# A decoder trunk on one core: pre-norm statistics by a tile of ones, and an opening of three units

## What is computed

```python
def rmsnorm(x, g):
    y = xf * lax.rsqrt(jnp.mean(xf * xf, axis=-1, keepdims=True) + RMS_EPS)
    return y * g
...
for l in range(DEPTH):
    h = h + 0.5 * rmsnorm(swiglu(rmsnorm(h, g[FFN1_PRE]), ffn_w_in[l, 0], ffn_w_out[l, 0]), g[FFN1_POST])
    hn = rmsnorm(h, g[MIX_PRE])
    ...
    h = h + rmsnorm(merged @ w_o[l], g[MIX_POST])
    h = h + 0.5 * rmsnorm(swiglu(rmsnorm(h, g[FFN2_PRE]), ffn_w_in[l, 1], ffn_w_out[l, 1]), g[FFN2_POST])
```

## Time and profile before

| | us |
|---|---|
| median of three runs | 1187.16 |
| the profiled execution | 1185.94 |
| its span, first to last instruction | 1184.1 |
| PE busy | 1174.6 |
| DVE busy | 727.6 |
| ACT busy | 554.6 |
| POOL busy | 428.5 |

### The profile page before, as it was taken

One profiled execution on the slowest core, in us unless ns is written; L12 is line 12 of the kernel. 1 busy time (PEld: TensorE's weight loads), 2 busy tenths in 40 slices (PEclk: granted clock), 3 DMA queues, 4 the chain that ended last, 5 costly groups with the idle time before them and its releaser, 6 DMA issues.

```text
span 1184.1 us, 23842 instructions
## 1 busy us (share of the span) xinstructions
PE 1174.6 (99%) x9265; PEld 1144.5 (97%) x9265; DVE 727.6 (61%) x1131; ACT 554.6 (47%) x809; POOL 428.5 (36%) x486
## 2 busy tenths in 40 slices
PE   9999999999999999999999999999999999999997
PEld 8999999999999999999999999999999999999986
DVE  5755445968666865544587554458676668755542
ACT  6533335536554643333455333346366546543441
POOL 0955500007212276542108545110073122955500
PEclk9999999999999999999999999999999999999999
DMA  9754357373355355535636553574733653654540
GB/s 324 260 178 155 130 184 221 107 236 98 90 156 187 122 196 171 174 128 183 214 111 213 176 168 120 196 212 132 235 105 90 186 170 120 222 192 159 194 161 35
DMA packets 197998, 198.70 MB, mean 168 GB/s; under 512 B 4368, under 2 KB 190864, under 8 KB 197920
## 3 DMA queue, kind: packets, MB, share of 16 engines
q1 hardware_dynamic: 197600, 197.27, 52.1%
q10 hardware_dynamic: 320, 0.34, 0.1%
HBM read 196.54 MB, written 1.05 MB: 167 GB/s over the span
## 4 chain that ended last, share of the span: by engine, by line
PE 94%; issue 3%; DVE 1%; ACT 1%; DMA 1%; POOL 0%; SPq 0%; DVEq 0%; ACTq 0%; POOLq 0%
PE bank L525 27%; PE bank L526 27%; PE bank L524 27%; PE bank L761 2%; PE bank L763 2%; PE bank L762 2%; PE bank L850 1%; PE bank L845 1%; DVE w_lo L1295 1%; PE bank L804 1%; PE bank L559 1%; PE bank L558 1%; DMA raw<-in_ffn_w_in 1%; PE bank L815 0%; PE bank L653 0%
## 5 line engine op out<-in xcount | busy, mean ns | idle before, releaser
L524 PE MATMUL bank<-x_hi,w_hi 128*128 128x272 f32 (+1 forms) x1993 | 574.1, 288 | 0.7 <-DVE w_lo L1718 0.7
L525 PE MATMUL bank<-x_lo,w_hi 128*128 128x272 f32 (+1 forms) x1993 | 572.6, 287 | 0.0
L526 PE MATMUL bank<-x_hi,w_lo 128*128 128x272 f32 (+1 forms) x1993 | 570.7, 286 | 0.0
L964 ACT ACTIVATE w_hi<-raw 128x2048 fp32r<-128x2048 f32 (+3 forms) x201 | 339.1, 1693 | 411.7 <-PE bank L526 397.2
L1295 DVE TENSOR_TENSOR w_lo<-raw,w_hi 128x2048 fp32r<-128x2048 f32 (+3 forms) x203 | 419.4, 2072 | 146.7 <-ACT w_hi L964 146.5
L524 PEld LDWEIGHTS bank<-x_hi,w_hi 128*128 128x128 f32 x1993 | 377.2, 189 | 2.0 <-DVE w_lo L1718 0.9
L525 PEld LDWEIGHTS bank<-x_lo,w_hi 128*128 128x128 f32 x1993 | 376.8, 189 | 0.3
L526 PEld LDWEIGHTS bank<-x_hi,w_lo 128*128 128x128 f32 x1993 | 375.0, 188 | 0.0
L1919 POOL TENSOR_TENSOR hid_hi<-silu,up_r 128x272 f32 x88 | 138.3, 1571 | 159.6 <-DVE up_r L1494 153.2
L525 PE MATMUL bank<-hid_lo,w_hi 128*128 128x272 f32 x528 | 152.5, 289 | 0.0
L526 PE MATMUL bank<-hid_hi,w_lo 128*128 128x272 f32 x528 | 152.1, 288 | 0.0
(11 more groups left out here) (217 smaller groups left out, 1318.5 us busy)
## 6 DMA issues: line engine op xcount, KB each, us to landing
raw<-in_ffn_w_in SPq DMA_DIRECT2D x86, 1024.0 KB, 5.0
raw<-in_w_in SPq DMA_DIRECT2D x24, 1024.0 KB, 5.6
raw<-in_ffn_w_out SPq DMA_DIRECT2D x24, 768.0 KB, 4.2
raw<-in_ffn_w_out SPq DMA_DIRECT2D x24, 640.0 KB, 3.9
raw<-in_ffn_w_out SPq DMA_DIRECT2D x10, 1024.0 KB, 4.9
raw<-in_w_in SPq DMA_DIRECT2D x16, 512.0 KB, 5.3
raw<-in_w_attn_proj SPq DMA_DIRECT2D x32, 256.0 KB, 4.6
raw<-in_w_o SPq DMA_DIRECT2D x8, 1024.0 KB, 5.6
```

Source lines behind the costliest of these rows:

```text
L524: pe.matmul(ps[:, t0:T], w[0], a_hi[:, t0:T], start=start, stop=False)
L525: pe.matmul(ps[:, t0:T], w[0], a_lo[:, t0:T], start=False, stop=False)
L526: return pe.matmul(ps[:, t0:T], w[1], a_hi[:, t0:T], start=False, stop=stop)
L964: last = act.activation(hi, w, ACT.Copy)
```

## The change

The three sums and three spreads of a pre-norm become one matmul: a 128x128 tile of ones times `acc` gives every partition the sum of every token (`sum_all`). DVE and ACT then compute the root at full width on all partitions (`pre_rms`, `pre_root`): scaled mean square, ACT's square root, two reciprocals, and a sum of 1/root and root/mean square, which corrects the root. POOL's power goes. Post-norms stay as they were.

The opening runs three units slice by slice (`first_three`), each slice as its data come: two pieces of one slice, then three of two. The second copy of the tokens isn't loaded; ACT squares the slices of `h` and DVE adds them (`first_square`, `first_adds`), and the sum stands ahead of slice 6. The warm-up is four matmuls of 256 columns on a tile that DVE zeroes first. The fourth unit follows on its own, its splits in halves.

```diff
-PIECES, PK = KD // 2, 2
+OPEN_K = (slice(0, 1), slice(1, 2), slice(2, 4), slice(4, 6), slice(6, 8))
+OPEN_UNITS = 3
+OPEN_BANKS = (3, 1, 6, 0, 4, 5)
+LAST_PIECE = len(OPEN_K) - 1
+FOURTH = (slice(0, KD // 2), slice(KD // 2, KD))
...
+def open_order(piece):
+    return (0, 2, 1) if OPEN_K[piece].stop == OPEN_K[piece].start + 1 else (0, 1, 2)
...
-            sp.dma_start(g_all[:, :], norm_columns).then_inc(norms_in, 16)
             first_w = ffn_w_in[0:1, 0].rearrange("o (k p) n -> p (o k) n", p=P)
-            first_to, second_to = (raw[:, u, :].rearrange("p (k c) -> p k c", c=UW) for u in range(2))
-            for piece in range(PIECES):
-                k = slice(PK * piece, PK * (piece + 1))
+            def columns(piece):
+                k = OPEN_K[piece]
                 sp.dma_start(h[:, k, :], x_columns[:, k, :]).then_inc(columns_in[piece], 16)
-                sp.dma_start(first_to[:, k, :], first_w[:, k, 0:UW]
-                             ).then_inc(raw_landed[0] if piece == PIECES - 1 else first_raw[piece], 16)
-                if piece % 2 == 1:
-                    k = slice(KD // 2 * (piece // 2), KD // 2 * (piece // 2 + 1))
-                    sp.dma_start(second_to[:, k, :], first_w[:, k, FF:FF + UW]
-                                 ).then_inc(second_raw if piece == 1 else raw_landed[1], 16)
+            def open_weights(piece):
+                k = OPEN_K[piece]
+                if k.stop == k.start + 1:
+                    kk = slice(k.start * UW, k.stop * UW)
+                    sp.dma_start(raw[:, 0:3:2, kk], first_w[:, k.start, 0:2 * UW].rearrange("p (u c) -> p u c", u=2)
+                                 ).then_inc(first_raw[piece][0], 16)
+                    sp.dma_start(raw[:, 1, kk], first_w[:, k.start, FF:FF + UW]).then_inc(first_raw[piece][1], 16)
+                    return
+                for u in range(OPEN_UNITS):
+                    c = u % 2 * FF + u // 2 * UW
+                    sp.dma_start(raw[:, u, :].rearrange("p (k c) -> p k c", c=UW)[:, k, :], first_w[:, k, c:c + UW]
+                                 ).then_inc(raw_landed[u] if piece == LAST_PIECE else first_raw[piece][u], 16)
+            for piece in range(len(OPEN_K)):
+                columns(piece)
+                open_weights(piece)
+            for half, k in enumerate(FOURTH):
+                sp.dma_start(raw[:, 3, :].rearrange("p (k c) -> p k c", c=UW)[:, k, :], first_w[:, k, FF + UW:FF + 2 * UW]
+                             ).then_inc((fourth_raw, raw_landed[3])[half], 16)
...
                         if (k, c) == SUM_AT:
-                            sum_part(q, l, 0)
-                        if (k, c) == SPREAD_AT:
-                            spread_rms(q, l)
+                            sum_all(q, l)
                         if c == 0 and k in EARLY_K[(q - 2) // 2 % 3]:
...
+            def first_three():
+                def product(c, k, low_weights, operand, start=False, stop=False):
+                    return pe.matmul(bank[OPEN_BANKS[c]][:, 0:T], weights(c // 2, k, c % 2)[low_weights], operand[:, k, :],
+                                     start=start, stop=stop)
+                pe.wait_ge(xhi_ready, 1)
+                pe.wait_ge(first_hi, 1)
+                for c in range(2):
+                    product(c, 0, 0, x_hi, start=True)
+                x_tile(0, 0)
+                for c in range(2):
+                    product(c, 0, 0, x_lo)
+                pe.wait_ge(first_lo, 1)
+                for c in range(2):
+                    product(c, 0, 1, x_hi)
+                for k in range(KD):
+                    piece = [k in range(s.start, s.stop) for s in OPEN_K].index(True)
+                    if k > 0:
+                        x_tile(k, 0)
+                    for at, u in enumerate(open_order(piece)):
+                        if k + at == 0:
+                            continue
+                        if k == OPEN_K[piece].start:
+                            if piece == LAST_PIECE:
                                 unit_split(u, 0)
+                            else:
+                                pe.wait_ge(first_lo, OPEN_UNITS * piece + at + 1)
+                        if (k, u) == OPEN_SUM_AT:
+                            pe.wait_ge(consts, 1)
+                            sum_all(0, 0)
+                        for c in (2 * u, 2 * u + 1):
+                            last = products(bank[OPEN_BANKS[c]], weights(u, k, c % 2), x_hi[:, k, :], x_lo[:, k, :],
+                                            k == 0, k == KD - 1, 0)
+                            if k == KD - 1:
+                                last.then_inc(first_done if c % 2 == 0 else unit_done, 1)
...
+            def fourth_unit():
+                pe.wait_ge(fourth_lo, 1)
                 for mt in range(2):
+                    if mt == 1:
+                        tile_free(T_FFN_IN[0] + 7, 0, 7)
                     for k in range(KD):
+                        if (mt, k) == (0, FOURTH[1].start):
+                            unit_split(3, 0)
+                        last = products(bank[2 + mt], weights(3, k, mt), x_hi[:, k, :], x_lo[:, k, :], k == 0, k == KD - 1, 0)
                     last.then_inc(first_done if mt == 0 else unit_done, 1)
...
+            def sum_all(q, l):
+                n = l * NORMS + q
+                pe.wait_ge(acc_done, adds_to(n + 1))
+                pe.matmul(small[:, S_BC:S_BC + T], ones[:, :], acc[:, :], start=True, stop=True).then_inc(ssq_done, 1)
...
-                pe.matmul(warm[:, :], ident[:, :], ident[:, :].unsqueeze(1).to_broadcast([P, 4, P]), start=True, stop=True)
-            for _ in range(WARM_SHORT):
-                pe.matmul(warm[:, 0:2 * P], ident[:, :], ident[:, :].unsqueeze(1).to_broadcast([P, 2, P]), start=True, stop=True)
+                pe.matmul(first_warm[:, 0:SEQ], r[:, 0:P], r[:, 0:SEQ], start=True, stop=True)
...
+            def pre_root(n):
+                act.wait_ge(pre_newton, n // 2 * 4 + 1)
+                act.activation(sq[:, 0, :], acc[:, :], ACT.Sqrt).then_inc(pre_root_done, 1)
...
-            act.dma_start(first_meta, meta_tokens).then_inc(tokens_in[2], 16)
+            act.dma_start(g_all[:, :], norm_columns).then_inc(norms_in, 16)
+            act.preload_act_table(ACT.Sqrt)
...
+            act.wait_ge(norms_in, 16)
+            for piece, ks in enumerate(OPEN_K):
+                act.wait_ge(columns_in[piece], 16)
+                for k in range(ks.start, ks.stop):
+                    first_operand(k)
+                for u in open_order(piece):
+                    open_split(u, piece)
+                for k in range(ks.start, ks.stop):
+                    first_square(k)
+            fourth_split(0)
+            fourth_split(1)
+            pre_root(0)
             act.preload_act_table(ACT.Silu)
...
-            def mean_square(q, l):
-                if l + q == 0:
-                    dve.wait_ge(first_sums_done, 3)
-                    dve.tensor_scalar(var[:, 0:2], first_sums[:, 0:2], 1.0 / D, EPS, ALU.mult, ALU.add)
-                    dve.tensor_scalar(var[0:META, 2:3], first_sums[0:META, 2:3], 1.0 / D, EPS, ALU.mult, ALU.add
-                                      ).then_inc(var_ready, 1)
-                    return
-                dve.wait_ge(ssq_done, l * NORMS + q + 2)
-                dve.tensor_scalar(var[:, 0:3], small[:, S_SUM:S_SUM + 3], 1.0 / D, EPS, ALU.mult, ALU.add
-                                  ).then_inc(var_ready, 1)
...
-            def take_rms(q, l):
-                dve.wait_ge(bcast_done, l * NORMS + q + 1)
-                dve.tensor_copy(r[:, :], small[:, S_BC:S_BC + T]).then_inc(r_ready, 1)
-                dve.wait_ge(r_ready, l * 3 + q // 2 + 1)
+            def pre_rms(q, l):
+                n = l * 3 + q // 2
+                dve.wait_ge(ssq_done, l * NORMS + q + 2)
+                dve.tensor_scalar(acc[:, :], small[:, S_BC:S_BC + T], POST / D, POST * EPS, ALU.mult, ALU.add
+                                  ).then_inc(pre_newton, 1)
+                dve.wait_ge(pre_newton, n * 4 + 1)
+                dve.reciprocal(sq[:, 1, :], acc[:, :]).then_inc(pre_newton, 1)
+                dve.wait_ge(pre_root_done, n + 1)
+                dve.reciprocal(r[:, :], sq[:, 0, :]).then_inc(pre_newton, 1)
+                dve.wait_ge(pre_newton, n * 4 + 2)
+                dve.tensor_tensor(sq[:, 1, :], sq[:, 1, :], sq[:, 0, :], ALU.mult).then_inc(pre_newton, 1)
+                dve.wait_ge(pre_newton, n * 4 + 4)
+                dve.tensor_tensor(r[:, :], r[:, :], sq[:, 1, :], ALU.add).then_inc(r_ready, 1)
+                dve.wait_ge(r_ready, n + 1)
...
+                for k in range(ks.start, ks.stop):
+                    x_low(0, g_all, k)
+                if piece > 0:
+                    first_adds(OPEN_K[piece - 1])
+                for at, u in enumerate(open_order(piece)):
+                    open_split(u, piece, at)
+            first_adds(OPEN_K[LAST_PIECE])
+            fourth_split(0)
```

(69 more changed lines are left out.)

181 lines of the change are left out of this document (52 added, 129 removed).

## The result

The changed kernel takes 1189.16 us, median of 22 runs (1188.31 to 1190.3); the kernel before, measured beside it, 1187.38, median of 22 (1185.53 to 1190.84). The ratio is 1.0017, 95% interval 1.0011 to 1.0023: slower by 1.8 us, a little less than the 0.2% that I had called just measurable. A later set gave 1189.32 beside 1186.96, ratio 1.0018 (1.0009 to 1.0028); the ratio leaves out one execution of 1260.21 us, in which the granted clock was 0.85 where the others have 0.997 to 1.0. The forecast was 1185.1, with 1182.0 to 1187.0. The profiled executions, 1185.94 before and 1189.08 after, lie 3.1 apart and their spans 3.0, because that of before lies 1.4 under the median of its kernel and that of after 0.1.

A forecast was written before the change was run, and what follows sets the result against it. It took PE as the bound, busy 1174.6 of 1184.1 us. The opening's 2.35 us gain less 0.2 at five boundaries, where DVE waits eat PE's 2.8 saved, gives 2.1 off 1187.16: 1185.1 us, range 1182.0 to 1187.0.

The forecast's parts named there:

- R: Time of one 128x272 reciprocal on DVE, two per pre-norm chain of 1.22 + 2R; taken as 1.36 us, 1.29 to 1.43.
- The bounds 0.43 and 2.6: Limits on R: below, a two-operand operation of that width, 0.43 us; above, 9 ns for each element, 2.6 us.
- The rest of the chain: DVE from the scale to r without the two reciprocals: scale, multiply, add, waits and overlaps, 1.22 us of 3.94.
- The mechanism: Later r delays DVE's in-order queue and PE waits; each 0.07 us in R moves the five boundaries' sum by 0.6.
- the five steps: Net change at the five pre-norms behind the opening: -0.1, +0.5, +0.1, -0.5, -0.3 us, given as -0.2 in sum.
- the ends of R and of the opening: Forecast time at the limits of R (1.29 to 1.43) and of the opening's gain (1.85 to 2.65): 1184.2 to 1186.2.
- rival (2): Reciprocal pays its step per element, 2.6 us; the five boundaries lose 12.5 us together: 1199.5, slower; chance 0.08.
- Statistics on PE: Five later pre-norms: sums and spreads of 5.06 us become matmuls of 0.46 each, 2.3, so PE saves 2.8 us.
- Who waits for r: Later r makes PE wait 0.2 to 0.9 us behind four of five boundaries, not behind layer 0's second FFN.
- The opening: First product near 5.1, unit 4 starting at 30.95 us against 33.29: 2.35 us gained, 1.85 to 2.65.
- Rival (3): Shorter warm-up and a pause delay PE's clock rise to near 10.7; opening gains only 0.85 us: 1186.5; chance 0.10.
- Rival (1): Reciprocal is pipelined like other DVE operations, 0.4 to 0.6 us; all 2.8 us count, 5.2 in all: 1182.0; chance 0.12.

The follow-up runs named there:

- the probe: Changed kernel with twelve reciprocals of different widths put ahead of DVE's first work, only to read their durations; the execution took 1196.71 us.
- the kernel with one reciprocal: Changed kernel without the root's correction: scale, ScalarE's root, one reciprocal as r; 1181.52 us beside 1186.57 for the kernel before, ratio 0.9959.

## Why the prediction was wrong

**The term that failed: R, the time of a 128x272 reciprocal.** "The widest row is nearest: (230 - 164)/15 = 4.4 ns an element, 164 + 271 x 4.4 = 1.36 us, which I take." Measured: 1.85 and 1.79. Both anchors of that slope were off the line. The 164 ns of one element lie 5 above it; the 230 ns of 16x16 were of 16 partitions, 13 less than with 128, and 10 less again than the 240 of the same shape in the probe, for which I have no cause. So 66 ns stood for what is 94 along the line, and 271 elements multiplied the error. The bounds 0.43 and 2.6 held the value; the range that I made of them, 1.29 to 1.43, was the spread of one reading of the same two rows, not the uncertainty between the rows. The rate from 16x16 was itself contradicted by the 9 ns from two to three elements, and I settled that for one side. The rest of the chain, 1.22 in the prediction (its own terms add up to 1.20), measured 4.80 - 3.65 = 1.15.

The Trainium skill, "VectorE: DVE Perf Modes", section "First, the fixed hardware budget", with its "repeat count of 8", stood for an estimate of 2.4 us; the measurement lies between that and my value, and decides: 6.25 ns an element.

**The mechanism was right.** The prediction's own rate, 0.6 us for each 0.07 in R, turns 1.82, the mean of the two, into 0.46 / 0.07 x 0.6 = 3.9 us more: 1185.1 + 3.9 = 1189.0, for 1189.16 measured. On the traces it is 1183.8 + 3.9 + 0.5 of the opening = 1188.2 for 1189.08. That the medians agree to 0.2 has luck in it: between the traces the boundaries cost 4.6 more than forecast and the opening gave 0.5 less, while the trace of before lies 1.4 under its median. Zero gain was put at R = 1.6 and a loss of over 0.2% at 1.8; by the prediction's own rate 1.8 makes 0.14%, and 0.17% came at 1.82. Two more of its small sums are off, without weight for the account: the five steps that it prints add up to -0.3, not -0.2, and the ends of R and of the opening to 1184.45 and 1186.45, not 1184.2 and 1186.2. So the outcome is rival (2)'s, at less than a third of its price (4.1 us above the forecast for 14.4).

**Statistics on PE.** Right: 0.46 for the sum, 2.7 (by the traces 2.9) saved for 2.8, shown by the kernel with one reciprocal.

**Who waits for r.** Right for four boundaries; the second FFN of layer 0 came to them, and in the mixer of layer 1 a second wait, 0.3 for the taken key tile. Both follow from the later `r`, as the sizes do.

**The opening.** The sign was right; 2.35 was 1.8, 1.7 in the second trace. The first product came at 4.68 (forecast 5.1), unit 4 at 31.57 (30.95). PE in time, opening:

```profile
11.06 0.36 PE L548 MATMUL bank<-x_hi,w_hi 128*128 128x272 f32 x1 [0.38 <-DVE w_lo L1740]
...
20.53 0.70 PE L682 MATMUL bank<-acc,ones 128*128 128x272 f32 x2 [0.20 <-DVE acc L1748]
...
31.57 0.29 PE L548 MATMUL bank<-x_hi,w_hi 128*128 128x272 f32 x1
```

Slice 2 starts 0.3 later than the forecast 10.75, the sum 0.5 later than 20.0. DVE in time shows both releasers:

```profile
10.23 1.89 DVE L1740 TENSOR_TENSOR w_lo<-raw,w_hi 128x512 fp32r<-128x512 f32 x3
...
19.40 0.98 DVE L1748 TENSOR_TENSOR acc<-acc,sq 128x272 f32<-128x272 f32 x2
```

The first low split of slice 2 ends at 10.9 (forecast 10.6), the last add at 20.4 (19.95): I had costed DVE's order there 0.3 to 0.4 too short. Rival (3) did not happen: from 7.50 on products start every 0.125 us, before it every 0.23. That this is where the prediction had it is luck: in the second trace of the changed kernel, behind the same warm-up, the step is 0.125 from 5.2 on. It changes little, as the prediction said of a rise up to a microsecond earlier, since PE then waits for the splits of slices 1 and 2 (0.7 and 0.35 us): unit 4 starts there at 31.70. Rival (1) did not happen.

## What to carry to other kernels

A rate worked out from rows of a few elements must not be multiplied by a few hundred: anchors with different partitions or at the floor of the instruction's time bend the slope, and where two pairs of rows give different rates, both belong in the range. One run with the wide instruction in it gives the price. Before a narrow operation is made wide to spare another engine a hand-over, write down how long the wide chain is on the engine that everybody waits for; here 2.7 us saved on PE were lost because a chain of DVE grew from 2.5 to 4.8 us at five places. Where the wide form is wanted all the same, replace a second reciprocal by products: here three of 0.44 us took the place of a reciprocal of 1.8, a multiply and an add, and the chain was 1.0 us shorter.
